# Cache compression read from half-chunk pages: 512 adjacent key columns per token offset, a key ring of four steps, and x kept on chip

## The reference

```python
def compress(k, w1, w2, pe):
    chunks = k[:, :n_chunk * CMP_STRIDE].reshape(B, n_chunk, CMP_STRIDE, N_KV_HEADS, HEAD_DIM)
    w1s = w1.reshape(CMP_SUB, CMP_STRIDE, HEAD_DIM, CMP_HID)      # CMP_SUB 2, CMP_STRIDE 16
    part = jnp.einsum('bcrkd,srdf->bcskf', chunks, w1s)
    nc = n_chunk - CMP_SUB + 1                                    # 128 chunks, 127 blocks
    h = part[:, 0:nc, 0]
    for s in range(1, CMP_SUB):
        h = h + part[:, s:s + nc, s]
    h = h + jnp.einsum('srd,srdf->f', pe.reshape(CMP_SUB, CMP_STRIDE, HEAD_DIM), w1s)
    return jax.nn.gelu(h) @ w2
```

## Time and profile before

| | us |
|---|---|
| median of 3 runs | 3756.75 |
| lowest, highest | 3750.2, 3764.89 |
| the profiled execution: span | 3758.4 |
| the profiled execution: its own time | not listed apart from the runs |
| busy: PE, DVE, ACT, POOL | 3512.7, 1484.1, 1150.6, 113.5 |
| DMA: bytes, mean rate | 615.57 MB, 164 GB/s |

### The profile page before, as it was taken

The page is one execution under the profiler, slowest core; times in us unless marked ns, Lnnn a source line. Parts: engine busy times, 40 slices in busy tenths (PEclk is TensorE's granted clock), DMA queues, the critical chain, the costliest instruction groups (busy, mean ns, idle before and its releaser), DMA issues.

```text
span 3758.4 us, 66365 instructions
## 1 busy us (share of the span) xinstructions
PE 3512.7 (93%) x24264; PEld 3272.8 (87%) x24264; DVE 1484.1 (39%) x2416; ACT 1150.6 (31%) x1736; POOL 113.5 (3%) x222
## 2 busy tenths in 40 slices
PE   6999999999899999999998877879979999999998
PEld 4888888888799999999997655559979999999997
DVE  2212122111355543433332554545454444444444
ACT  3222222221233333233332432233334333342332
POOL 0000000000000000000000002220000000000000
PEclk9999999999899999999997778889989999999999
DMA  7565555655356654444443047874434444444442
GB/s 247 181 215 172 181 180 177 216 175 175 113 184 199 200 179 156 150 152 132 138 154 102 21 136 247 292 250 160 162 112 134 156 142 148 154 141 152 151 135 79
DMA packets 533879, 615.57 MB, mean 164 GB/s; under 512 B 17712, under 2 KB 495601, under 8 KB 532465
## 3 DMA queue, kind: packets, MB, share of 16 engines
q1 hardware_dynamic: 518002, 544.61, 45.3%
q0 software_dynamic: 15760, 69.59, 5.3%
HBM read 600.63 MB, written 30.01 MB: 168 GB/s over the span
## 4 chain that ended last, share of the span: by engine, by line
PE 88%; DVE 3%; DMA 3%; issue 2%; ACT 2%; SPq 2%; DVEq 0%; ACTq 0%; POOL 0%; PEldq 0%; POOLq 0%
PE bank L1172 18%; PE bank L1174 18%; PE bank L1173 18%; PE bank L1127 6%; PE bank L1128 6%; PE bank L1129 6%; PE bank L1093 3%; PE bank L1105 2%; DMA sb_krow<-in_cache_nsa_kv 1%; PE bank L1305 1%; PE bank L1362 1%; PE bank L1281 1%; PE bank L1346 1%; PE bank L1208 1%; SPq L532 1%
## 5 line engine op out<-in xcount | busy, mean ns | idle before, releaser
L1172 PE MATMUL bank<-sb_act_hi,sb_w_hi 128*128 128x320 f32 x3200 | 994.8, 311 | 47.2 <-DVE sb_act_lo L1567 36.2
L1540 DVE TENSOR_TENSOR sb_w_lo<-sb_raw,sb_w_hi 128x1024 fp32r<-128x1024 f32 x592 | 723.5, 1225 | 755.5 <-ACT sb_w_hi L803 749.1
L1173 PE MATMUL bank<-sb_act_hi,sb_w_lo 128*128 128x320 f32 x3200 | 993.7, 311 | 0.0
L1174 PE MATMUL bank<-sb_act_lo,sb_w_hi 128*128 128x320 f32 x3200 | 993.5, 310 | 0.0
L803 ACT ACTIVATE sb_w_hi<-sb_raw 128x1024 fp32r<-128x1024 f32 x592 | 623.1, 1055 | 773.1 <-PE bank L1174 763.5
L1172 PEld LDWEIGHTS bank<-sb_act_hi,sb_w_hi 128*128 128x128 f32 x3200 | 605.3, 189 | 49.1 <-issue 41.3
L1173 PEld LDWEIGHTS bank<-sb_act_hi,sb_w_lo 128*128 128x128 f32 x3200 | 605.1, 189 | 0.0
L1174 PEld LDWEIGHTS bank<-sb_act_lo,sb_w_hi 128*128 128x128 f32 x3200 | 605.1, 189 | 0.0
L1492 DVE TENSOR_TENSOR sb_keyT_lo<-bank,sb_keyT_hi 128x512 fp32r<-128x512 f32 x256 | 173.0, 690 | 734.3 <-ACT sb_keyT_hi L756 733.1
L1127 PE MATMUL bank<-sb_keyT_hi,sb_w_hi 128*128 128x256 f32 x1024 | 424.9, 415 | 9.0 <-DVE sb_keyT_lo L1492 9.0
L1128 PE MATMUL bank<-sb_keyT_hi,sb_w_lo 128*128 128x256 f32 x1024 | 414.7, 405 | 0.0
(11 more groups left out here) (335 smaller groups left out, 3364.4 us busy)
## 6 DMA issues: line engine op xcount, KB each, us to landing
sb_raw<-in_w_mlp SPq DMA_DIRECT2D x64, 2048.0 KB, 8.5
sb_raw<-in_w_in SPq DMA_DIRECT2D x60, 2048.0 KB, 8.2
sb_ada_raw<-in_w_ada SPq DMA_DIRECT2D x48, 2048.0 KB, 9.0
sb_pages<-in_cache_nsa_kv SPq DMA_DIRECT2D x512, 128.0 KB, 2.5
sb_krow<-in_cache_nsa_kv SPq DMA_DIRECT2D x128, 256.0 KB, 5.1
sb_vrow<-in_cache_nsa_kv POOLq DMA_DIRECT2D x128, 256.0 KB, 5.7
sb_raw<-in_w_conv_proj SPq DMA_DIRECT2D x8, 2048.0 KB, 8.1
sb_raw<-in_w_attn_proj SPq DMA_DIRECT2D x8, 2048.0 KB, 8.1
```

The source lines that it names most:

```text
L1172: mm(out, w_hi[:, buf, k, :], x_hi[:, kk, :], start=(kk == 0), stop=False)
L1173: mm(out, w_lo[:, buf, k, :], x_hi[:, kk, :], start=False, stop=False)
L1174: last = mm(out, w_hi[:, buf, k, :], x_lo[:, kk, :], start=False, stop=(kk == KT - 1))
L1540: V.tensor_tensor(w_lo[:, buf], raw[:, (t // 2) % 2, CH * ch:CH * ch + CH, P * (t % 2):P * (t % 2) + P], w_hi[:, buf].bitcast(F32), ALU.su ...
```

## The change

The unit is now a kind: four heads at once. A token's row of one kind is 2 KB over the four heads, and the half of a chunk (8 tokens) becomes the thing that lies on a partition: `half_chunks` views a page as 16 half-chunks of 8 tokens. Half h of the loads brings tokens 4h to 4h+3 of every half-chunk; one page is a transfer of 16 partitions (eight apart, one of 8 slots for the page) x 4 tokens x 2 KB. A step i (0 to 7) transposes, for token offset i, 2 page groups t x 4 heads into two banks (`keys_turn`), whose columns are head, chunk, half, slot. ACT and DVE take each bank apart into the two halves rh (`key_part`, `bank_part`: two operations of 256 columns a bank), in an order in which chunks of a head stand side by side. Then offset r = 16 s + 8 rh + i needs the 512 adjacent columns from s on: 4 (rh, s) x 3 = 12 matmuls of 512 columns a step, 96 a kind, all into one bank. Keys stand in a ring of four steps (`KRING`). The panels' products stand at steps 1 and 4 and behind step 7.

The smaller tiles no longer cover `mx`: x stays there, the reload goes, and so does the second panel's wait. x is still written to DRAM for later. Stores of the compressed rows are one a kind, of all four heads.

```diff
-        keyT_hi = at("keyT_hi", [P, 2, KEYS], A_HI + 65536, F32R)
-        pages = at("pages", [P, 2, NPAGE, 2 * HD], A_RING)
+        KRING, KROW = 4, NKV * P + 8
+        keyT_hi = at("keyT_hi", [P, KRING, 2, KROW], A_T + 6144, F32R)
+        pages = at("pages", [P, 2, 2, 4, KVW], A_RING)
...
+        half_chunks = A["cache_nsa_kv"][0].rearrange("g (q r) k h d -> g q r k (h d)", r=CSTR // 2)
...
+        def key_part(keys, i, rh, t):
+            return keys[:, i % KRING, rh, 0:NKV * P].rearrange("p (h t s c) -> p h t c s", h=NKV, t=2, s=8)[:, :, t]
+        def bank_part(i, t, rh):
+            return bank[2 * (i % 2) + t][:, :].rearrange("p (h c r s) -> p h r c s", h=NKV, r=2, s=8)[:, :, rh]
...
-            def unit_pages(b, u, page):
+            def unit_pages(b, kind, half, page):
-                sp.wait_ge(s_kt_bank, b * 32 + 8 * u - 8 + 2 * CREDIT)
-                for pg in range(NPAGE):
-                    sp.dma_start(pages[:, pair, pg, :],
-                                 cache[ds(page[pg], 1), :, kind, 256 * pair:256 * pair + 256].rearrange("a p n -> p (a n)")).then_inc(s_page[pair], 16)
+                sp.wait_ge(s_kt_bank, b * 32 + 16 * kind + 8 * half - 8 + 2 * CREDIT)
+                for t in range(2):
+                    for slot in (0, 4, 1, 5, 2, 6, 3, 7):
+                        sp.dma_start(pages[slot:P:8, half, t, :, :],
+                                     half_chunks[ds(page[8 * t + slot], 1), :, 4 * half:4 * half + 4, kind, :].rearrange("a q r n -> (a q) r n")
+                                     ).then_inc(s_page[half], 16)
...
-                    if u < 2 or not last:
-                        unit_pages(b, u + 2, page)
-                    for p in ((2 * u + 2, 2 * u + 3) if u < (2 if last else 3) else ()):
-                        ada_panel(b, p)
+                    for half in range(2):
+                        if kind == 0:
+                            unit_pages(b, 1, half, page)
+                        elif not last:
+                            unit_pages(b + 1, 0, half, page)
+                        if half == 0:
+                            ada_panel(b, 3 * kind + 2)
+                        elif not (last and kind):
+                            ada_panel(b, 3 * kind + 3)
+                            ada_panel(b, 3 * kind + 4)
...
-            sp.dma_start(x0_a[:, :, :], x_d[:, 0:12, :]).then_inc(s_xld, 16)
-            sp.dma_start(x0_b[:, :, :], x_d[:, 12:16, :]).then_inc(s_xld, 16)
...
-                act.activation(keyT_hi[:, u % 2, 512 * f:512 * f + 512], bank[f % 4][:, :], ACT.Copy).then_inc(s_kt_hi, 1)
+                    act.wait_ge(s_kt_mm, b * 16 + 8 * kind + i + 1 - KRING + CREDIT)
+                    for rh in range(2):
+                        last = act.activation(key_part(keyT_hi, i, rh, t), bank_part(i, t, rh), ACT.Copy)
+                    last.then_inc(s_kt_hi, 1)
...
+                    for i in range(8):
+                        if i in (1, 4):
+                            ada_prod(3 * kind + i // 4)
+                        elif i in (2, 5):
+                            ada_turn(3 * kind + i // 4)
+                        pe.wait_ge(s_kt_ev, b * 32 + 16 * kind + 2 * i + 2 + CREDIT)
+                        if i < 7:
+                            turn_ahead(i)
...
+                        for rh in range(2):
+                            for s in range(CLEN // CSTR):
+                                r = s * CSTR + 8 * rh + i
+                                k_hi, k_lo = (k[:, i % KRING, rh, s:s + NKV * P] for k in (keyT_hi, keyT_lo))
+                                mm(hout, w1_hi[:, kind, r, :], k_hi, start=(i + rh + s == 0), stop=False)
...
+                    ada_prod(3 * kind + 2)
+                    turn_ahead(7)
+                    pe.wait_ge(s_gelu, b * 2 + kind + 1 + CREDIT)
```

More of the change, by code:

```diff
@@ new lines, in compress_act, with ada_row_out @@
+            def compress_act(b, last):
+                def ada_row_out(p):
+                    act.wait_ge(s_ada_pe, b * 6 + p + 1 + CREDIT)
+                    act.activation(ada_row[:, :], bank[7][:, 0:256], ACT.Copy).then_inc(s_ada_row, 1)
+                for kind in range(2):
+                    for i in range(8):
+                        if i in (1, 4):
+                            ada_row_out(3 * kind + i // 4)
+                        if i == 7:
+                            act.wait_ge(s_kt_mm, b * 16 + 8 * kind + 8 + CREDIT)
+                            act.wait_ge(s_cmp_o, b * 2 + kind + CREDIT)
+                            act.activation(gelu[:, :, :], bank[4 + kind][:, :].rearrange("p (h c) -> p h c", h=NKV), ACT.Gelu_apprx_tanh,
+                                           bias=pe_col[:, kind:kind + 1]).then_inc(s_gelu, 1)
+                            ada_row_out(3 * kind + 2)
+                        if i < 6:
+                            keys_hi(b, kind, i + 2)
+                        elif kind == 0:
+                            keys_hi(b, 1, i - 6)
+                        elif not last:
+                            keys_hi(b + 1, 0, i - 6)
@@ L1141, in compress_pe @@
                     if kind == 0:
[L1142 removed]
+                        last = mm(bank[6][:, 0:NKV * NC_S].rearrange("p (h c) -> p h c", h=NKV), w2[:, 0, :], gelu[:, :, 0:NC_S], start=True, stop=True)
                     else:
[L1144 to L1146 removed]
+                        for hh in range(NKV):
+                            last = mm(bank[6][0:NC_S, P * hh:P * hh + P], gelu[:, hh, 0:NC_S], w2[:, 1, :], start=True, stop=True)
@@ L1147, in compress_pe @@
                     last.then_inc(s_cmp_o, 1)
-            for f in range(8):
-                keys_bank(0, 0, f)
+                    ada_turn(3 * kind + 2)
+            keys_turn(0, 0, 0)
+            keys_turn(0, 0, 1)
             pe.wait_ge(s_w1_lo, 3)
@@ new lines, in keys_lo, with ada_out @@
+            def keys_lo(b, kind, i):
+                for t in range(2):
+                    dve.wait_ge(s_kt_hi, b * 32 + 16 * kind + 2 * i + t + 1)
+                    for rh in range(2):
+                        last = V.tensor_tensor(key_part(keyT_lo, i, rh, t), bank_part(i, t, rh), key_part(keyT_hi, i, rh, t).bitcast(F32),
+                                               ALU.subtract)
+                    last.then_inc(s_kt_ev, 1)
+            def compress_dve(b, last):
+                def ada_out(p):
+                    dve.wait_ge(s_ada_t, b * 6 + p + 1)
+                    V.tensor_tensor(ada[:, ds(b * 12 + 2 * p, 2), :],
+                                    bank[7][:, 0:32].rearrange("p (a c) -> p a c", a=2)[:, :, 0:NSEQ],
+                                    b_ada[:, ds(b * 12 + 2 * p, 2)].unsqueeze(2).to_broadcast([P, 2, NSEQ]), ALU.add).then_inc(s_ada_ev, 1)
+                for kind in range(2):
+                    for i in range(8):
+                        if i in (2, 5):
+                            ada_out(3 * kind + i // 4)
+                        if i < 6:
+                            keys_lo(b, kind, i + 2)
+                        elif kind == 0:
+                            keys_lo(b, 1, i - 6)
+                        elif not last:
+                            keys_lo(b + 1, 0, i - 6)
+                    dve.wait_ge(s_cmp_free[kind], b + CREDIT)
+                    dve.wait_ge(s_cmp_o, b * 2 + kind + 1 + CREDIT)
```

197 lines of the change are left out of this document (70 added, 127 removed).

## The result

The changed kernel takes **3540.4 us** (median of 4 runs, 3527.91 to 3543.44) for 3758.81 before: a ratio of 0.9413, interval 0.9396 to 0.9431. It is faster, by 218 us; 3421 was forecast and 3395 to 3490 given as the range, so the time lies above it. The profiled execution is the shortest of the four: in the prompt's attention, far behind this stage, it took 161.4 us at a granted clock of 0.82, for 175.0 at 0.73 in the one profiled before.

A forecast was written before the change was run, and what follows sets the result against it. PE was taken to bound the compression stage, 58.2 us a pair. With 37.6, its end came to 66.8 − 3.5 + 16 × 37.6 − 1.6 = 663 us for 998.6, 335.5 less: 3421 us, range 3395 to 3490.

The forecast's parts named there:

- Matmuls: Compression stage: 96 matmuls of 512 adjacent columns a pair at 0.226 us, 21.7 us, 20.5 less than before.
- PE's own sum: Compression stage: PE's matmuls, transposes, panels and w2 products, 21.7 + 6.5 + 7.8 + 1.0 = 37.0 us a pair.
- D: Key matmuls: a column costs the same in either layout, pair 57.5 us, time 3740 us; chance 0.06.
- The circle: PE work, SP's 16 page issues, then the step 1 panel's landing: 20.0 + 8.2 + 0.4 + 9.0 = 37.6 us a pair.
- the price of a page transfer: SP's queue: 0.51 us issue distance as lower end, 2.5 us of one landing as far upper end.
- Rival B: Page transfers pace the pair: at 0.7 us each 40.6 us, 3469; at 0.8 42.2 us, 3495; chance 0.20.
- The queue is not the bound by itself: SP's queue: page numbers 9.3 us, page transfers 16.4 and three panels take 27 of 37 us a pair.
- x on chip: Dropping x's reload and the second weight panel's wait for modulate gains nothing.
- Evictions: Bank split on ACT and DVE: 1.5 and 1.7 us a step of 4.6 us, hidden.
- under 0.5 us: Sign to check in the changed kernel's timeline: ACT's and DVE's split under 0.5 us an operation.
- rival C: The split, writing with a step of 8, paces the pair: at 1.25 us each 41.5 us, 3483; chance 0.05.
- E: Slower: page transfers starve PE from 1.02 us each; at 1.25 the pair takes 65.5 us, 3874; chance 0.05.

The follow-up runs named there:

- Kernel 8: Against the change: matmuls read a constant tile, three each a step without a gap and with steps of 2, 4 and 16 elements; 3674.56 us.
- kernel 3: Against the change: a page lands on 16 adjacent partitions instead of 16 that stand eight apart; 3642.26 us.
- kernel 4: Against the change: a page transfer reads one run of 8 KB for each partition instead of four of 2 KB; 3535.31 us.
- kernel 1: Against the change: SP issues the panel of step 1 ahead of the 16 page transfers of half 1; 3548.8 us.
- 11: Against the change: SP's list written out, so page numbers are read once and the loop's end goes, order kept; 3537.51 us.
- kernel 13: Against kernel 10: ACT and DVE split each bank into plain halves of 256 adjacent columns, without the step of 8 elements; 3413.48 us.
- Kernel 10: Against the change: panels issued on ACT's queue, and SP's list written out with page numbers read once; 3423.74 us.
- kernel 6: Against kernel 1: SP reads no page numbers inside the loop; every sequence reads the pages of four numbers read at the start; 3426.09 us.
- kernel 9: Against the change: panel of step 1 ahead of half 1's pages, and SP's list written out with page numbers read once; 3449.4 us.

## Why the prediction was wrong

- **Matmuls: right.** 0.235 us for 512 columns, at the upper bound given (0.226 taken): 96 x 0.009 = 0.9 us a pair. PE's own sum, 37.0, is 37.6 in the run where it waits for nothing. Kernel 8 rules out D.
- **The circle: right in kind.** The wait is for the panel at step 1, behind SP's 16 page transfers of half 1, as the prediction had it; 20.0 + 8.2 + 0.4 + 9.0 beside the two rounds of the chain shows where it was too small. What it did not have is the stretch that stands on SP's list alone.
- **The step that failed first** is the price of a page transfer: "I take the issue distance, 0.51 us, as the lower end", and the sum took it for the value. It is 0.74: 16 issues took 12.2 us, with what stands between them, for 8.2. The landing side's step of eight does it (kernel 3). That the price sits in the circle, kernel 4 bears out: 61 ns less an issue, 16 x 0.061 = 1.0 us, and a pair 1.7 us shorter. Rival B covered that price, 29.4 + 16 x 0.74 = 41.2 us a pair.
- **The term that was left out**: a late panel costs more than the wait. The product and the transposes behind it ran at the lower clock, 1.7 + 0.9 = 2.6 us inside the circle; PE's part of it was 23.1 us for 20.0; the rest is about what 48 matmuls at 0.009 us more each add, 0.4 us. With 4.0 for the issues, 3.1 for PE and 1.0 for the landing (9.1 and 11.6 in the two rounds, for 9.4), 37.6 becomes 45.7; measured 45.4.
- **"The queue is not the bound by itself"** was wrong once the transfer cost 0.74. I counted 27 us of SP a pair, with 16.4 for pages, 9.3 for page numbers (the two rows named for it are 9.5 apart) and no term for the loop's end. Measured are 23.7 for pages, 10.7 for numbers and 5 to 6 for the loop's end in every second pair; 44.7 us of slack were left in 550, and with the panel ahead of the pages none at all (kernel 1). Kernels 1 and 11 undo one cause each and gain nothing that can be told (+8 and -3 us); with both undone (9) the time falls by 91.
- **x on chip: right**, nothing. The first dense product stands behind a wait for DVE of 13.17 us, for 13.05 before:

```profile
794.52 0.60 PE L1190 MATMUL bank<-sb_act_hi,sb_w_hi 128*128 128x320 f32 x1 [13.17 <-DVE sb_act_lo L1590]
```

- **Evictions: right** on the sum: 0.73 us an operation on ACT and 0.67 on DVE, hidden where PE doesn't wait (kernel 13). The mark "under 0.5 us" was wrong, and the 1.9 that rival C weighed came out at 1.9 on ACT and 1.6 on DVE. **E** needed 1.02 us a transfer and falls.
- **The range**: its top, 3490, came from B's times, 3469 to 3495, which held transfers of 0.7 to 0.8 us but PE at full clock behind its waits.

Kernel 10, with slack on SP's list, takes 3423.74 us: the forecast of 3421 was about the time of PE's own work, which the change does not reach. That kernel 6's pair is 37.6 us, the very figure forecast, is luck: there it is PE's work alone, with dearer matmuls, and in the forecast it was the circle over SP.

## What to carry to other kernels

When a change makes the bounding engine quicker, count every issuing queue again at the new pace: each transfer, each register read and each wait in it, with the time that the queue had to spare before as a row of its own (here 249.5 us of 550, then 44.7). A wait that PE runs into can be paid twice, by its length and by the clock of the work behind it, so price it with both: here the panel's product took 3.64 us behind 4.10 us of waiting, and still 1.93 behind 1.40 us of waiting in kernel 9. And undo causes in pairs: two causes in a row each show nothing when one alone is undone.
